# Mixture-of-experts stage of a two-model forward pass: both unit sizes in one block, unrolled groups, tokens as partitions in the small units' down product

## The chip, the cores and the metric

One core of one Trainium2 chip runs the whole program in one launch. The metric is the device time of an execution in microseconds (us). Before the change three runs took 4977.19, 4983.99 and 4990.39 us, median 4983.99 us.

## The reference, cut to what matters

The program is a chain of two small models over 512 tokens of width 1024. The change touches one layer of the first: a top-2-of-8 mixture of SwiGLU experts, in float32, each expert 1024 by 3584.

```python
def moe_swiglu(h, w_router, w_gate, w_up, w_down):
    xt = h.reshape(b * t, d)                              # 512 x 1024
    top_logits, top_idx = lax.top_k(xt @ w_router, 2)     # of 8
    gates = jax.nn.softmax(top_logits, axis=-1)
    order = jnp.argsort(top_idx.reshape(-1))
    xs = xt[order // 2]                                   # 1024 rows, by expert
    hid = (jax.nn.silu(lax.ragged_dot(xs, w_gate, sizes))
           * lax.ragged_dot(xs, w_up, sizes))             # 3584 wide
    ys = lax.ragged_dot(hid, w_down, sizes)               # back to 1024
    ...                                                   # weighted sum of each token's two rows
```

## The kernel before, in words

`moe1` (L1701) runs a norm, `route_stage`, then `swiglu_stage` (L1016) twice, each a block of its own with a barrier and its own buffers, then `combine_stage`. The router counts the tokens of each expert and cuts them into **units**. An expert with at most 128 tokens is one unit of size 0 (128 rows, called A here). A larger one becomes units of size 1 (152 rows, B). How many there are is known only on the chip, so every engine reads the count (`units`, L1725) and loops over the units with `Fori`. With these inputs there are 5 units of A and 3 of B: the trace has 70 groups of one form and 42 of the other.

A unit reads all of its expert's weights, 3 x 3584 x 1024 floats, in 14 **groups** of 256 hidden columns. A group has 1 MB of gate weights, 1 MB of up weights and 1 MB of down weights, in one of two buffers `b`. `groups` (L1041) is an inner `Fori` of seven turns of two groups. For one group:

- SP waits until the buffer is free (`freed[b]`, given by TensorE after the group's last matmul) and issues three DMAs (L1062 to L1064). They add 48 to `loaded[b]`.
- TensorE waits for `loaded[b]`, then for each half j of 128 hidden columns runs the gate and up products over 8 slices of width (L1093) into banks 4 to 7. Here the weights are the stationary operand and `xu`, the unit's rows turned so that width lies in partitions, moves with 128 or 152 columns. Each float32 `matmul` of the program is two TensorE records and two weight-load records in the trace.
- ScalarE applies silu (L1125), VectorE multiplies by the up product (L1141) and so makes `hid[j]`.
- TensorE multiplies down (L1100): for each j eight matmuls with a 128 x 128 piece of `wd` stationary and `hid` moving, into banks 0 to 3, two of them per bank, the output transposed (width in partitions). Zero matmuls (L1076) open these banks at the start of a unit, because they are filled with start=False.

Around the groups stands the **boundary** of a unit. After the last group VectorE copies the four banks to `yT` (L1148), TensorE turns them back to rows (L1112), VectorE copies them to `yrow` (L1684), ScalarE's queue stores them to DRAM (L1689) and waits until they have landed. The next unit begins with `ExpertRows.turn` (L1664, the gathered rows are turned on TensorE) and `place` (L1675, VectorE copies them into `xu` with the norm's gain). POOL's `fetch` (L1647 the index list, L1651 the gather of rows) runs a unit ahead: it waits only for the turn of the unit before.

The order within a queue is the program's. The lines that the change and the steps of the prediction touch:

```python
with sp.Fori(0, units(sp)) as u: ...                                # L1052
sp.wait_ge(freed[b].sem, freed[b].at(u * per[b] + i))               # L1057
pe.wait_ge(loaded[b].sem, loaded[b].at((u * per[b] + i + 1) * 48))  # L1087
```

The dense feed-forward stage `ffn_stage` is used for comparison. It has the same three loads per group but 256 rows at a time, its groups are written out without a loop, and its down product (L1242) has `hid` stationary and 512 columns of `wd` moving.

Of the kernel before, what the change touches and what calls it, by code (L numbers as in the profile page):

```python
# [22 lines left out]
P = 128  # L23
T = 512
TT = T // P
D = 1024
# [11 lines left out]
ROWS_MAX = (FIRST_ROW[1] + UNITS_MAX[1] * UNIT_ROWS[1] + P - 1) // P * P  # L38
LEVELS = 7
# [145 lines left out]
def settle(eng, passed):  # L185


    eng.sem_inc(passed.sem, 1)
# [822 lines left out]
def row_parts(rows):  # L1011

    return [(r0, min(P, rows - r0)) for r0 in range(0, rows, P)]


def swiglu_stage(S, name, letter, rows, hidden, units, weights, x_of, gather, emit):  # L1016

    nc, ps = S.nc, S.ps  # L1020
    n_groups = hidden // GROUP
    per = ((n_groups + 1) // 2, n_groups // 2)
    subs = row_parts(rows)
    per_unit = 2 * len(subs)
    sig = lambda x: S.sig(letter + x)
    loaded = [sig("loaded0"), sig("loaded1")]
    hidden_ready = [sig("hidden0"), sig("hidden1")]
    gate_up, gated = [sig("gate_up0"), sig("gate_up1")], [sig("gated0"), sig("gated1")]
    freed = [sig("freed0"), sig("freed1")]
    y_ready, y_taken, y_turned, emitted, zeros_ready = (  # L1030
        sig(x) for x in ("y_ready", "y_taken", "y_turned", "emitted", "zeros"))
    with ExitStack() as st:
        wg = S.sb(name + "_wg", [P, 2, KD, GROUP], F32, st)
        wu = S.sb(name + "_wu", [P, 2, KD, GROUP], F32, st)
        wd = S.sb(name + "_wd", [P, 2, 2, D], F32, st)
        gated_sb = S.sb(name + "_gs", [P, 2, rows], F32, st)
        hid = S.sb(name + "_hid", [P, 2, rows], F32, st)
        yT = S.sb(name + "_yt", [P, KD, rows], F32, st)
        zero = S.sb(name + "_zero", [P, BANK], BF16, st)

        def groups(eng, u, body):  # L1041

            with eng.Fori(0, n_groups // 2) as i:
                for b in range(2):
                    body(i, b)
            if n_groups % 2:
                body(n_groups // 2, 0)

        with nc.Block(name) as block:
            @block.sync  # L1050
            def _(sp):
                with sp.Fori(0, units(sp)) as u:  # L1052
                    g, up, dn = weights(sp, u)

                    def body(i, b):

                        sp.wait_ge(freed[b].sem, freed[b].at(u * per[b] + i))  # L1057
                        f = (i * 2 + b) * GROUP
                        gv = g[:, bass.ds(f, GROUP)].rearrange("(k p) f -> p k f", p=P)
                        uv = up[:, bass.ds(f, GROUP)].rearrange("(k p) f -> p k f", p=P)  # L1060
                        dv = dn[bass.ds(f, GROUP), :].rearrange("(j p) d -> p j d", p=P)
                        sp.dma_start(wg[:, b, :, :], gv).then_inc(loaded[b].sem, 16)  # L1062
                        sp.dma_start(wu[:, b, :, :], uv).then_inc(loaded[b].sem, 16)
                        sp.dma_start(wd[:, b, :, :], dv).then_inc(loaded[b].sem, 16)  # L1064
                    groups(sp, u, body)

            @block.tensor
            def _(pe):
                pe.wait_ge(zeros_ready.sem, zeros_ready.at(1))
                with pe.Fori(0, units(pe)) as u:  # L1070
                    if gather is not None:
                        gather.turn(pe, u)

                    pe.wait_ge(y_taken.sem, y_taken.at(u))
                    for b in range(4):
                        nc.tensor.matmul(ps[b][:, :], zero[:, 0:P], zero[:, :], start=True, stop=False,  # L1076
                                         skip_group_check=True)
                    if gather is None:
                        pe.wait_ge(emitted.sem, emitted.at(per_unit * u))
                    else:  # L1080
                        pe.wait_ge(gather.x_ready.sem, gather.x_ready.at(per_unit * (u + 1)))

                    settle(pe, S.sig("passed_pe"))

                    def body(i, b):
                        pe.wait_ge(loaded[b].sem, loaded[b].at((u * per[b] + i + 1) * 48))
                        n = u * n_groups + i * 2 + b  # L1087
                        for j in range(2):

                            pe.wait_ge(hidden_ready[j].sem, hidden_ready[j].at(n))  # L1090
                            for w, bank in ((wg, 4 + j), (wu, 6 + j)):
                                for k in range(KD):
                                    last = nc.tensor.matmul(ps[bank][:, 0:rows], w[:, b, k, j * P:(j + 1) * P], x_of(k, u),  # L1093
                                                            start=(k == 0), stop=(k == KD - 1))
                            last.then_inc(gate_up[j].sem, 1)
                        for j in range(2):
                            pe.wait_ge(hidden_ready[j].sem, hidden_ready[j].at(n + 1))
                            for d in range(KD):
                                at = (d % 2) * rows
                                last = nc.tensor.matmul(ps[d // 2][:, at:at + rows], wd[:, b, j, d * P:(d + 1) * P],  # L1100
                                                        hid[:, j, :], start=False, stop=False, skip_group_check=True)
                        last.then_inc(freed[b].sem, 1)
                    groups(pe, u, body)
                    nc.tensor.matmul(ps[3][0:32, 0:2], zero[:, 0:32], zero[:, 0:2], start=False, stop=True,
                                     skip_group_check=True).then_inc(y_ready.sem, 1)
                    pe.wait_ge(y_taken.sem, y_taken.at(u + 1))
                    pe.wait_ge(hidden_ready[0].sem, hidden_ready[0].at((u + 1) * n_groups))
                    pe.wait_ge(hidden_ready[1].sem, hidden_ready[1].at((u + 1) * n_groups))
                    for s, (r0, n) in enumerate(subs):
                        for half in range(2):  # L1110
                            for kk in range(4):
                                last = nc.tensor.transpose(ps[4 + 2 * s + half][0:n, kk * P:(kk + 1) * P],  # L1112
                                                           yT[:, 4 * half + kk, r0:r0 + n], S.const("ident"))
                            last.then_inc(y_turned.sem, 1)

            @block.scalar
            def _(act):
                with act.Fori(0, units(act)) as u:
                    def body(i, b):
                        n = u * n_groups + i * 2 + b  # L1120
                        for j in range(2):
                            act.wait_ge(gate_up[j].sem, gate_up[j].at(n + 1))

                            act.wait_ge(hidden_ready[j].sem, hidden_ready[j].at(n))
                            nc.scalar.activation(gated_sb[:, j, :], ps[4 + j][:, 0:rows], ACT.Silu).then_inc(gated[j].sem, 1)  # L1125
                    groups(act, u, body)
                    if gather is not None:
                        gather.store(act, u)

            @block.vector  # L1130
            def _(dve):
                nc.vector.memset(zero[:, :], 0.0).then_inc(zeros_ready.sem, 1)
                with dve.Fori(0, units(dve)) as u:
                    if gather is not None:
                        gather.place(dve, u)

                    def body(i, b):
                        n = u * n_groups + i * 2 + b
                        for j in range(2):
                            dve.wait_ge(gated[j].sem, gated[j].at(n + 1))  # L1140
                            nc.vector.tensor_tensor(hid[:, j, :], gated_sb[:, j, :], ps[6 + j][:, 0:rows],  # L1141
                                                    ALU.mult).then_inc(hidden_ready[j].sem, 1)
                    groups(dve, u, body)
                    dve.wait_ge(y_ready.sem, y_ready.at(u + 1))

                    dve.wait_ge(y_turned.sem, y_turned.at(per_unit * u))
# [4 lines left out]
                    if gather is not None:  # L1151
                        gather.before_emit(dve, u)
# [1753 lines left out]
```

## Time and profile before

| | us |
|---|---|
| runs | 4977.19, 4983.99, 4990.39 |
| the profiled execution, its own time | 4991.39 |
| its span, first to last instruction | 4989.7 |
| TensorE busy over the span | 3590.2 (72%) |
| VectorE, ScalarE, POOL busy | 1889.2, 579.9, 1363.7 |
| router's blocks end, expert stage begins | about 1484 |
| first and last weight load of the expert stage on TensorE | 1501.3 to 2876.7 |
| combine's first gather | 2885.67 |

The profile cuts the span in 40 slices of 124.7 us. The expert stage fills slices 12 to 22, in which TensorE's digit is 9 but for one. What follows it, slices 23 to 39, is the second model, which the change does not touch.

### The profile page before, as it was taken

The page shows a single profiled execution, that of the slowest core. Times are in us where ns is not written, and L with a number is a line of the kernel's source. Part 1 is how long each engine was busy: PE and PEld are TensorE (multiplying, and loading weights), DVE is VectorE, ACT ScalarE, POOL GpSimd, SP SyncE. Part 2 cuts the span into 40 slices and gives each one's busy share as a digit, 9 for nine tenths or more (in the row PEclk, how much of TensorE's full clock was granted, in tenths as well). Part 3 has the DMA queues.
Part 4 walks back from the last instruction along what each step waited for, and adds up shares of the span by engine and source line. Part 5 has one row for each costly group of instructions (what it writes and reads, how often), then busy time and mean ns, then how long its engine had stood idle before and what let it go on. Part 6 is the DMA issues. An engine that isn't in the chain of part 4 may idle for free. (4 is left out here: it accounts for less than half of the span.)

```text
span 4989.7 us, 48641 instructions
## 1 busy us (share of the span) xinstructions
PE 3590.2 (72%) x18469; PEld 2608.9 (52%) x18469; DVE 1889.2 (38%) x3706; ACT 579.9 (12%) x1313; POOL 1363.7 (27%) x1167
## 2 busy tenths in 40 slices
PE   7969999997569999998999959966065055046036
PEld 3455777645439999998999934643022022012012
DVE  2051230115710000000000031728787777777764
ACT  1121000122301010100000011421011011001001
POOL 0020000002310000000000000004777877877875
PEclk9969999898779999998999979788587578578579
DMA  3112774210138788876776721016899999999998
GB/s 107 51 38 94 247 244 154 88 68 1 39 144 278 271 278 287 274 269 229 253 244 237 247 88 51 1 72 235 291 367 353 327 360 352 322 351 371 327 354 349
DMA packets 533096, 1086.83 MB, mean 218 GB/s; under 512 B 36950, under 2 KB 317808, under 8 KB 532864
## 3 DMA queue, kind: packets, MB, share of 16 engines
q1 hardware_dynamic: 378100, 522.81, 30.7%
q0 software_dynamic: 150544, 545.64, 29.8%
q10 hardware_dynamic: 4348, 17.07, 0.8%
q8 instruction: 56, 0.92, 0.1%
q14 instruction: 48, 0.39, 0.0%
HBM read 1064.14 MB, written 21.28 MB: 218 GB/s over the span
## 5 line engine op out<-in xcount | busy, mean ns | idle before, releaser
L2408 PE MATMUL bank<-peer_ring,peer_diag 128*128 128x512 f32 x1024 | 519.8, 657 | 938.9 <-ACT peer_diag L2505 559.3
L2408 PEld LDWEIGHTS bank<-peer_ring,peer_diag 128*128 128x128 f32 x1024 | 203.1, 208 | 1255.2 <-ACT peer_diag L2505 891.7
L2268 POOL DMA_INDIRECT peer_ring<-in_peer_u_dram,peer_expert x512 | 666.2, 1301 | 686.4 <-DVE peer_expert L2582 486.5
L2647 DVE SCALAR_TENSOR_TENSOR peer_ring<-peer_ring,h_rows 128x1024 f32<-128x1024 f32 x512 | 596.7, 1222 | 177.3 <-DMA peer_ring<-in_peer_u_dram,peer_expert 176.0
L2268 POOL DMA_INDIRECT peer_ring<-in_peer_v_dram,peer_expert x512 | 549.5, 1073 | 160.8 <-issue 154.9
L1141 DVE TENSOR_TENSOR experts_hid<-experts_gs,bank 128x128 f32<-128x128 f32 (+1 forms) x224 | 66.6, 297 | 1216.3 <-ACT experts_gs L1125 1216.3
L1093 PE MATMUL bank<-rows_xt,experts_wg 128*128 128x128 f32 (+1 forms) x3584 | 470.3, 285 | 14.3 <-DMA experts_wd<-in_moe_w_down_dram 13.8
L1093 PE MATMUL bank<-rows_xt,experts_wu 128*128 128x128 f32 (+1 forms) x3584 | 460.3, 282 | 0.0
L1093 PEld LDWEIGHTS bank<-rows_xt,experts_wg 128*128 128x128 f32 x3584 | 446.6, 194 | 24.6 <-issue 24.6
L1100 PE MATMUL bank<-experts_hid,experts_wd 128*128 128x128 f32 (+1 forms) x3584 | 442.0, 282 | 0.0
L1093 PEld LDWEIGHTS bank<-rows_xt,experts_wu 128*128 128x128 f32 x3584 | 440.1, 191 | 0.0
L1100 PEld LDWEIGHTS bank<-experts_hid,experts_wd 128*128 128x128 f32 x3584 | 431.9, 191 | 0.0
L2694 DVE SCALAR_TENSOR_TENSOR peer_acc<-peer_ring,peer_wgt,peer_acc 128x1024 f32<-128x1024 f32 x256 | 328.9, 1285 | 211.5 <-DMA peer_ring<-in_peer_v_dram,peer_expert 203.0
L401 PE MATMUL bank<-xT,proj_w 128*128 128x512 f32 (+2 forms) x736 | 325.0, 600 | 9.0 <-PEq L215 9.0
L1647 POOL DMA_DIRECT2D rows_index<-token_of_row x11 | 6.3, 572 | 991.8 <-PE bank L1664 664.6
L846 POOL TENSOR_TENSOR hgrn_both<-k,hgrn_diff 128x256 f32<-128x256 f32 x56 | 50.5, 908 | 827.2 <-ACT hgrn_diff L791 804.8
L404 PE MATMUL bank<-proj_w,xT 128*128 128x512 f32 (+2 forms) x704 | 265.6, 536 | 0.0
L401 PEld LDWEIGHTS bank<-xT,proj_w 128*128 128x128 f32 (+2 forms) x736 | 136.9, 187 | 190.6 <-issue 189.8
L404 PEld LDWEIGHTS bank<-proj_w,xT 128*128 128x128 f32 x704 | 127.0, 195 | 140.6 <-issue 140.4
L1125 ACT ACTIVATE experts_gs<-bank 128x128 f32<-128x128 f32 (+1 forms) x224 | 63.9, 285 | 966.2 <-PE bank L1093 965.8
L1232 PE MATMUL bank<-xT,ffn_wg 128*128 128x256 f32 x704 | 162.3, 384 | 1.3 <-ACT ada_c L1271 1.3
L1232 PE MATMUL bank<-xT,ffn_wu 128*128 128x256 f32 x704 | 159.1, 379 | 0.0
(421 smaller groups left out, 3446.5 us busy)
## 6 DMA issues: line engine op xcount, KB each, us to landing
experts_wg<-in_moe_w_gate_dram SPq DMA_DIRECT2D x112, 1024.0 KB, 5.2
experts_wu<-in_moe_w_up_dram SPq DMA_DIRECT2D x112, 1024.0 KB, 7.7
experts_wd<-in_moe_w_down_dram SPq DMA_DIRECT2D x112, 1024.0 KB, 9.4
ada_w<-in_w_ada_dram SPq DMA_DIRECT2D x12, 2048.0 KB, 8.0
ffn_wg<-in_ffn_w_gate_dram SPq DMA_DIRECT2D x22, 1024.0 KB, 6.8
ffn_wu<-in_ffn_w_up_dram SPq DMA_DIRECT2D x22, 1024.0 KB, 9.5
ffn_wd<-in_ffn_w_down_dram SPq DMA_DIRECT2D x22, 1024.0 KB, 11.6
proj_w<-in_c_w_in_dram SPq DMA_DIRECT2D x8, 2048.0 KB, 9.2
```

Of the source, the lines that this page charges most:

```text
L401: last = nc.tensor.matmul(out_of(g), wk[:, m * P:m * P + width], xT[:, k, :], start=(k == 0), stop=(k == KD - 1))
L404: last = nc.tensor.matmul(out_of(g), xT[:, k, m * P:(m + 1) * P], wk[:, 0:n], start=(k == 0), stop=(k == KD - 1))
L846: nc.gpsimd.tensor_tensor(halves(both[:, n % 2, :], l)[0], halves(k(p), l)[0], halves(diff[:, p % 2, l, :], l)[0], ALU.mult).then_inc(mixe ...
L1093: last = nc.tensor.matmul(ps[bank][:, 0:rows], w[:, b, k, j * P:(j + 1) * P], x_of(k, u), start=(k == 0), stop=(k == KD - 1))
L1100: last = nc.tensor.matmul(ps[d // 2][:, at:at + rows], wd[:, b, j, d * P:(d + 1) * P], hid[:, j, :], start=False, stop=False, skip_group_c ...
L1125: nc.scalar.activation(gated_sb[:, j, :], ps[4 + j][:, 0:rows], ACT.Silu).then_inc(gated[j].sem, 1)
L1141: nc.vector.tensor_tensor(hid[:, j, :], gated_sb[:, j, :], ps[6 + j][:, 0:rows], ALU.mult).then_inc(hidden_ready[j].sem, 1)
L1232: last = nc.tensor.matmul(ps[bank][:, 0:ROWS], w[:, b, k, j * P:(j + 1) * P], xT[:, k, u * ROWS:(u + 1) * ROWS], start=(k == 0), stop=(k = ...
L2268: pool.indirect_dma_start(out=ring[:, b, :], out_offset=None, in_=tables[phase], in_offset=bass.IndirectOffsetOnAxis(ap=G.expert[:, t, i * ...
L2408: last = nc.tensor.matmul(ps[hf][:, :], diag[:, b // 2, :], ring[:, b, hf * 512:(hf + 1) * 512], start=False, stop=(b == B - 1), skip_grou ...
L2647: nc.vector.scalar_tensor_tensor(ring[:, b, :], ring[:, b, :], 1.0, h2[:, t, :], ALU.mult, ALU.mult, accum_out=dots[:, b:b + 1]).then_inc( ...
L2694: nc.vector.scalar_tensor_tensor(acc[:, :], ring[:, b, :], wgt[:, i * B + b:i * B + b + 1], acc[:, :], ALU.mult, ALU.add).then_inc(weighed ...
```

## The change

One block replaces the two. All buffers of both sizes are allocated together, with one set of weight buffers, and SP goes from the last unit of A to the first of B without a barrier; for B it waits that A's groups have freed the buffer too. The inner loop is gone on all engines but SP: the 14 groups of a unit are written out, inside the loop over units. In A the rows of the next unit are turned inside the last group (into banks 2 and 3), one unit beyond the last as well. A's down product has `hid` stationary and 512 columns of `wd` moving, into banks 0 and 1, so its result has tokens in partitions; `yT`, its turning and the zero matmuls are gone in A. In B the next unit's rows are turned before the results are turned back, and the zero matmuls stand in the first group. Stores are no longer waited for unit by unit.

The old `swiglu_stage` is removed whole. New or changed, cut to its core:

```diff
+LISTED = ROWS_MAX + 2 * P
...
     def turn(self, pe, u):
...
         pe.wait_ge(self.gathered.sem, self.gathered.at(16 * len(self.subs) * (u + 1)))
-        pe.wait_ge(self.emitted.sem, self.emitted.at(2 * len(self.subs) * u))
...
     def store(self, act, u):
         for s, (r0, n) in enumerate(self.subs):
-            act.wait_ge(self.emitted.sem, self.emitted.at(2 * len(self.subs) * u + 2 * s + 2))
             act.dma_start(self.R.y[...], self.yrow[0:n, s, :]).then_inc(self.stored.sem, 16)
-        act.wait_ge(self.stored.sem, self.stored.at(16 * len(self.subs) * (u + 1)))
+def experts_stage(S, R):
+    n_groups = E_FF // GROUP
+    per = n_groups // 2
+    last = n_groups - 1
...
+            @block.sync
+            def _(sp):
+                def unit(E, size, u, others=None, n_others=0):
+                    e = expert_values(sp, R.expert[0:1, size, bass.ds(u, 1)], 0, N_EXP - 1)
...
+                    with sp.Fori(0, per) as i:
+                        for b in range(2):
+                            if others is not None:
+                                sp.wait_ge(others.freed[b].sem, others.freed[b].at(n_others * per))
+                                settle(sp, S.sig("passed_sp"))
+                            sp.wait_ge(E.freed[b].sem, E.freed[b].at(u * per + i))
...
+                            sp.dma_start(wg[:, b, :, :], gv).then_inc(E.loaded[b].sem, 16)
+                            sp.dma_start(wu[:, b, :, :], uv).then_inc(E.loaded[b].sem, 16)
+                            sp.dma_start(wd[:, b, :, :], dv).then_inc(E.loaded[b].sem, 16)
+                n_a, n_b = A.units(sp), B.units(sp)
+                with sp.Fori(0, n_a) as u:
+                    unit(A, 0, u)
+                with sp.Fori(0, n_b) as u:
+                    unit(B, 1, u, A, n_a)
...
+            @block.tensor
+            def _(pe):
+                n_a, n_b = A.units(pe), B.units(pe)
+                A.turn(pe, 0)
+                with pe.Fori(0, n_a) as u:
+                    pe.wait_ge(A.x_ready.sem, A.x_ready.at(2 * u + 2))
+                    for g in range(n_groups):
+                        b = g % 2
+                        pe.wait_ge(A.loaded[b].sem, A.loaded[b].at((u * per + g // 2 + 1) * 48))
+                        gate_up(A, u, g, 0)
+                        gate_up(A, u, g, 1)
+                        if g == last:
+                            A.turn(pe, u + 1)
+                        for j in range(2):
+                            pe.wait_ge(A.hidden[j].sem, A.hidden[j].at(u * n_groups + g + 1))
+                            if g == 0 and j == 0:
+                                pe.wait_ge(A.y_taken.sem, A.y_taken.at(u))
+                            for hf in range(2):
+                                ins = nc.tensor.matmul(ps[hf][:, :], hid[:, j, 0:P], wd[:, b, j, hf * 512:(hf + 1) * 512],
+                                                       start=(g == 0 and j == 0), stop=(g == last and j == 1))
+                        ins.then_inc(A.freed[b].sem, 1)
+                B.turn(pe, 0)
+                pe.wait_ge(A.y_taken.sem, A.y_taken.at(n_a))
+                pe.wait_ge(A.x_ready.sem, A.x_ready.at(2 * n_a + 2))
+                pe.wait_ge(zeros.sem, zeros.at(1))
+                with pe.Fori(0, n_b) as u:
+                    pe.wait_ge(B.x_ready.sem, B.x_ready.at(4 * u + 4))
+                    for g in range(n_groups):
...
+                        if g == 0:
+                            pe.wait_ge(B.emitted.sem, B.emitted.at(4 * u))
+                            for bank in range(4):
+                                nc.tensor.matmul(ps[bank][:, :], zero[:, 0:P], zero[:, :], start=True, stop=False,
+                                                 skip_group_check=True)
...
+                    B.turn(pe, u + 1)
+                    pe.wait_ge(B.y_taken.sem, B.y_taken.at(u + 1))
+                    for s, (r0, n) in enumerate(B.subs):
+                        for half in range(2):
+                            for kk in range(4):
+                                ins = nc.tensor.transpose(ps[2 * s + half][0:n, kk * P:(kk + 1) * P],
+                                                          yT[:, 4 * half + kk, r0:r0 + n], S.const("ident"))
+                            ins.then_inc(B.y_turned.sem, 1)
...
+            @block.scalar
+            def _(act):
+                with act.Fori(0, n_a) as u:
+                    for g in range(n_groups):
+                        silu(A, u, g, 0)
+                        silu(A, u, g, 1)
+                    act.wait_ge(A.y_taken.sem, A.y_taken.at(u + 1))
+                    A.store(act, u)
...
+                with act.Fori(0, n_b) as u:
...
+                    act.wait_ge(B.emitted.sem, B.emitted.at(4 * u + 4))
+                    B.store(act, u)
...
+            @block.vector
+            def _(dve):
+                A.place(dve, 0)
+                with dve.Fori(0, n_a) as u:
+                    for g in range(n_groups):
+                        hidden(A, u, g, 0)
+                        hidden(A, u, g, 1)
+                    A.place(dve, u + 1)
+                    dve.wait_ge(A.freed[1].sem, A.freed[1].at(u * per + per))
+                    dve.wait_ge(A.stored.sem, A.stored.at(16 * u))
+                    for hf in range(2):
+                        ins = nc.vector.tensor_copy(A.yrow[:, 0, hf * 512:(hf + 1) * 512], ps[hf][:, :])
+                    ins.then_inc(A.y_taken.sem, 1)
+                B.place(dve, 0)
+                with dve.Fori(0, n_b) as u:
...
+                    for bank in range(4):
+                        ins = nc.vector.tensor_copy(yT[:, 2 * bank:2 * bank + 2, :], ...)
+                    ins.then_inc(B.y_taken.sem, 1)
+                    B.place(dve, u + 1)
+                    dve.wait_ge(B.stored.sem, B.stored.at(32 * u))
+                    ...                                   # B.yrow copies, each after its y_turned
+            @block.gpsimd
+            def _(pool):
+                n_a, n_b = A.units(pool), B.units(pool)
+                A.fetch(pool, 0)
+                with pool.Fori(0, n_a) as u:
+                    A.fetch(pool, u + 1)
+                B.fetch(pool, 0)
+                with pool.Fori(0, n_b) as u:
+                    B.fetch(pool, u + 1)
```

## Rows read from the trace of the kernel before

**Rows 1.** The page's 40 slices, TensorE's busy tenths.

```profile
PE   7969999997569999998999959966065055046036
```

**Rows 2.** Timeline, a turn of A's inner loop: start, us, engine, line, operation [idle before].

```profile
1543.43 3.65 PEld L1100 LDWEIGHTS bank<-experts_hid,experts_wd 128*128 128x128 f32 x32
...
1547.73 2.05 PE L1093 MATMUL bank<-rows_xt,experts_wg 128*128 128x128 f32 x16 [0.45 <-DMA experts_wd<-in_moe_w_down_dram]
```

**Rows 3.** Timeline, SP's queue, A: the first load of a group.

```profile
1677.59 0.38 SPq L1062 DMA_DIRECT2D experts_wg<-in_moe_w_gate_dram  x1
1688.37 0.37 SPq L1062 DMA_DIRECT2D experts_wg<-in_moe_w_gate_dram  x1
1699.67 0.38 SPq L1062 DMA_DIRECT2D experts_wg<-in_moe_w_gate_dram  x1
...
1840.61 0.38 SPq L1062 DMA_DIRECT2D experts_wg<-in_moe_w_gate_dram  x1
```

**Rows 4.** Timeline, SP's queue, B: the first load of a group.

```profile
2387.81 0.37 SPq L1062 DMA_DIRECT2D experts_wg<-in_moe_w_gate_dram  x1
2400.23 0.38 SPq L1062 DMA_DIRECT2D experts_wg<-in_moe_w_gate_dram  x1
2412.61 0.37 SPq L1062 DMA_DIRECT2D experts_wg<-in_moe_w_gate_dram  x1
```

**Rows 5.** Timeline, the feed-forward stage: two weight loads that follow each other.

```profile
719.15 0.19 PEld L1242 LDWEIGHTS bank<-ffn_wd,ffn_hid 128*128 128x128 f32 x1 [0.24 <-issue]
719.58 0.19 PEld L1242 LDWEIGHTS bank<-ffn_wd,ffn_hid 128*128 128x128 f32 x1 [0.24 <-issue]
```

**Rows 6.** DMA view of 12 us each: 1513:1525, then 1558:1570 (us to landing stands last).

```profile
q8 instruction: 1, 0.02, 0.6%
...
experts_wd<-in_moe_w_down_dram SPq DMA_DIRECT2D x1, 1024.0 KB, 10.7
...
experts_wd<-in_moe_w_down_dram SPq DMA_DIRECT2D x1, 1024.0 KB, 9.4
```

**Rows 7.** The feed-forward stage, 600 to 900: busy time by engine, then the instruction queue.

```profile
600.00:900.00 300.00, 300.00 (x1170) 221.56 (x1169) 59.53 (x97) 11.14 (x29) 0.00 (x0) 1.00 0.57 195
...
q8 instruction: 9, 0.15, 0.2%
```

**Rows 8.** Timeline, a boundary of A, TensorE: its first and its last row.

```profile
1657.90 0.09 PEld L1104 LDWEIGHTS bank<-experts_zero 128*32 128x32 bf16 x1
...
1665.86 2.35 PEld L1093 LDWEIGHTS bank<-rows_xt,experts_wg 128*128 128x128 f32 x16 [0.63 <-issue]
```

**Rows 9.** DMA view: small transfers, us from issue to landing.

```profile
router_w<-in_moe_router_dram SPq DMA_DIRECT2D x1, 32.0 KB, 2.2
rows_index<-token_of_row POOLq DMA_DIRECT2D x8, 0.5 KB, 4.8
```

**Rows 10.** Timeline, from A's block to B's, TensorE's rows.

```profile
2308.21 0.09 PEld L1104 LDWEIGHTS bank<-experts_zero 128*32 128x32 bf16 x1
...
2335.11 4.30 PEld L1093 LDWEIGHTS bank<-rows_xt,experts_wg 128*128 128x128 f32 x16 [0.28 <-issue]
```

**Rows 11.** Timeline, a boundary of B: TensorE's and VectorE's rows.

```profile
2511.51 0.09 PEld L1104 LDWEIGHTS bank<-experts_zero 128*32 128x32 bf16 x1 [0.16 <-issue]
...
2511.81 1.62 DVE L1148 COPY experts_yt<-bank 128x304 f32<-128x304 f32 x4 [3.69 <-PE bank L1104]
...
2513.66 1.96 PE L1112 MATMUL bank<-consts,experts_yt 128*128 128x128 f32 x16 [1.97 <-DVE experts_yt L1148]
2514.35 2.47 DVE L1684 COPY rows_y<-bank 128x512 f32<-128x512 f32 x4 [0.92 <-PE bank L1112]
...
2516.97 1.67 PE L1664 MATMUL bank<-consts,rows_x 128*128 128x128 f32 x16 [1.35 <-DVE rows_y L1684]
2517.63 1.62 DVE L1675 TENSOR_TENSOR rows_xt<-bank,columns 128x512 f32<-128x512 f32 x4 [0.81 <-PE bank L1664]
...
2519.89 2.11 PEld L1093 LDWEIGHTS bank<-rows_xt,experts_wg 128*128 128x128 f32 x16 [0.78 <-issue]
```

More of the change, by code:

```diff
@@ L1005, in head_norm_stage @@
             s.base += n
[L1011 to L1146, printed above, removed]
-                    for b in range(4):
-                        ins = nc.vector.tensor_copy(yT[:, 2 * b:2 * b + 2, :],
-                                                    ps[b][:, 0:2 * rows].rearrange("p (d r) -> p d r", d=2))
-                    ins.then_inc(y_taken.sem, 1)
-                    if gather is not None:
-                        gather.before_emit(dve, u)
-                    for s, (r0, n) in enumerate(subs):
-                        for half in range(2):
-                            dve.wait_ge(y_turned.sem, y_turned.at(per_unit * u + 2 * s + half + 1))
-                            emit(u, s, half, ps[4 + 2 * s + half][0:n, :]).then_inc(emitted.sem, 1)
-            if gather is not None:
-                @block.gpsimd
-                def _(pool):
-                    with pool.Fori(0, units(pool)) as u:
-                        gather.fetch(pool, u)
@@ L1483, in route_stage @@
         token_i = S.sb("router_token", [P, TT], I32, st)
-        zero_rows = S.sb("router_zero", [1, ROWS_MAX], I32, st)
+        zero_rows = S.sb("router_zero", [1, LISTED], I32, st)
         blank = S.sb("router_blank", [P, D], F32, st)
@@ L1631, in __init__, with units @@
         self.rows, self.row0 = UNIT_ROWS[size], FIRST_ROW[size]
-        self.xg = S.sb(f"rows{size}_x", [P, 2, D], F32, st)
+        self.subs = [(r0, min(P, self.rows - r0)) for r0 in range(0, self.rows, P)]
+        self.bank0 = (2, 4)[size]
+        n = len(self.subs)
+        self.xg = S.sb(f"rows{size}_x", [P, n, D], F32, st)
         self.xu = S.sb(f"rows{size}_xt", [P, KD, self.rows], F32, st)
-        self.yrow = S.sb(f"rows{size}_y", [P, 2, D], F32, st)
-        self.index = S.sb(f"rows{size}_index", [P, 2], I32, st)
-        self.subs = row_parts(self.rows)
+        self.yrow = S.sb(f"rows{size}_y", [P, n, D], F32, st)
+        self.index = S.sb(f"rows{size}_index", [P, n], I32, st)
         self.indexed, self.gathered = (S.sig(f"e{size}_{x}", pool_dma=True) for x in ("indexed", "gathered"))
         self.turned, self.stored, self.x_ready = (S.sig(f"e{size}_{x}") for x in ("turned", "stored", "x_ready"))
-        self.emitted = S.sig(f"s{size}_emitted")
+        sig = lambda x: S.sig(f"s{size}_{x}")
+        self.loaded, self.freed = [sig("loaded0"), sig("loaded1")], [sig("freed0"), sig("freed1")]
+        self.hidden, self.gate_up, self.gated = ([sig(x + "0"), sig(x + "1")] for x in ("hidden", "gate_up", "gated"))
+        self.y_taken = sig("y_taken")
+        if size:
+            self.y_ready, self.y_turned, self.emitted = sig("y_ready"), sig("y_turned"), sig("emitted")
+    def units(self, eng):
+        size = 0 if self.row0 == 0 else 1
+        return expert_values(eng, self.R.units[0:1, size:size + 1], 1, UNITS_MAX[size])
     def fetch(self, pool, u):
-        S, nc, R = self.S, self.S.nc, self.R
-        pool.wait_ge(self.turned.sem, self.turned.at(2 * len(self.subs) * u))
+        S, nc, R, n_subs = self.S, self.S.nc, self.R, len(self.subs)
+        pool.wait_ge(self.turned.sem, self.turned.at(2 * n_subs * u))
         settle(pool, S.sig("passed_pool"))
@@ L1663, in turn @@
                     c = (4 * half + kk) * P
-                    last = nc.tensor.transpose(S.ps[4 + 2 * s + half][:, kk * P:kk * P + n], self.xg[0:n, s, c:c + P],
+                    last = nc.tensor.transpose(S.ps[self.bank0 + 2 * s + half][:, kk * P:kk * P + n], self.xg[0:n, s, c:c + P],
                                                S.const("ident")[0:n, 0:n])
@@ L1711, in moe1 @@
         R.y = nc.dram_tensor("y_rows", (ROWS_MAX, D), F32, kind="Internal").ap()
[L1712 removed]
+        R.token_of_row = nc.dram_tensor("token_of_row", (LISTED, 1), I32, kind="Internal").ap()
         norm_stage(S, "norm3", S.gains[:, 3, :], xn_dram=R.xn)
         route_stage(S, R)
[L1715 to L1726 removed]
+        experts_stage(S, R)
         combine_stage(S, R)
```

105 lines of the change are left out of this document (85 added, 20 removed).

## The prediction, made before the changed kernel was run

> **What bounds the kernel now.** I read the page's slices first, to place the stage: TensorE is at nine tenths through it [rows 1]. The gain has to come from what still lies between its matmuls, so I then read three timelines.
>
> Inside A's inner loop the 32 weight loads of a down product take 3.65 us [rows 2]. Taking off the last one's own 0.19 [rows 5] leaves a step of 0.112, so the 96 records of a group are 10.72 us. In SP's queue the first loads of successive groups stand 10.78 and 11.30 us apart, 22.08 for two groups [rows 3]. Two groups of matmuls are 21.44, so TensorE waits 0.64 per pair. The wait is named as one for the down weights [rows 2]. In B the same two steps are 12.42 and 12.38 [rows 4], which is the bare matmul time of 152 columns, with only 0.04 at the loop's edge. So the edge of the short loop is almost free, and A's 0.64 is the weight load's latency. A buffer is refilled only after its own group has ended, and is needed one group later. From the end of a group to the moment when the next group of that buffer may start passes 10.72 + 0.64 = 11.36 us. A therefore runs at the pace "one group's matmuls plus 11.36" per pair, and what shortens a group by x brings x per pair, not 2x.
>
> The boundaries are the rest: 8.0 us in A [rows 8], 8.4 in B [rows 11], and 26.9 from A's last product to B's first, because the second block loads weights and gathers rows from nothing [rows 10].
>
> **Part by part.**
>
> *A's down product.* Eight records of 512 columns instead of 32 of 128. In the feed-forward stage such records start 0.43 us apart [rows 5], so 3.44 instead of 3.57: a group becomes 10.59, a unit's fourteen 148.3.
>
> *The unrolled body.* The feed-forward stage is written out, and in 300 us it drew nine packets of 16 KB on the instruction queue for 1170 + 1169 TensorE records [rows 7], one per 260 records. A unit of A becomes 14 x 144 + 16 = 2032 records, 8 packets, and with its waits I take 9; a unit of B (2720) takes 11. What a packet does to a load can be read: a load of A during which one instruction packet ran landed its down weights after 10.7 us, one without after 9.4 [rows 6]. That is 1.3 us, on the very latency that sets A's pace. With an ordinary load the wait per pair is 11.36 - 10.59 = 0.77, with one hit by a packet 2.07. Seven pairs all ordinary wait 5.4, all hit 14.5; with nine of fourteen hit, 11.2. About 1.0 of it disappears beside the turn and the edge at the boundary, which leaves 10.2. B has 12.38 per group against 11.36 for a load: an ordinary load costs nothing, a hit one (12.66, and 0.1 for SP's second wait) 0.4 per pair, at most 2.7 a unit. I take 1.8, or 5.4 for three units.
>
> [...]
>
> *The far edge.* At the end of a unit's body TensorE now branches back over some 130 KB. No row shows such a branch. The near one costs 0.04 [rows 4], which is the lower bound; the upper is the landing of a small DMA under load, 4.8 us, while a small one alone lands in 2.2 [rows 9]. The records queued ahead of the branch cover part of it. I take 1.5, and keep 0 and 5. [...]
>
> *A's boundary.* Next rows are turned inside the last group: eight transposes, half of the 16 that take 1.67 [rows 11], 0.9 with their fill. VectorE's `place` and its two copies lie beside the last down product and the next gate products. Queued behind ScalarE's new wait for `y_taken` are the store and the next unit's first silu, wanted 3.6 us into the unit, while the copies end after 1.8; nothing is late. POOL has fetched those rows a unit earlier. A unit's period becomes 148.3 + 0.9 + 10.2 + 1.5 = 160.9, against 1840.61 - 1677.59 = 163.0 [rows 3]. Four boundaries save 8.4. The last unit, to its last product, goes from 163.0 - 8.0 = 155.0 to 159.4, which costs 4.4; the first saves 0.4 of zero matmuls. **A: -4.4.**
>
> *From A to B.* SP loads B's first groups during A's last, and the rows are there, since POOL runs ahead. What is left is B's turn (1.7) beside VectorE's two copies (about 1.4), then `place` (1.62) [rows 11], with semaphores 3.5. **-23.4.**
>
> *B.* After the last product the turn (1.67) runs beside the four copies (1.62), then the result's transposes (1.96): about 4.2 with the steps between, while `place` ends earlier [rows 11]. The zero matmuls move into the first group but stay, 1.0, and the far edge adds 1.5: 6.7 against 8.4, twice: -3.4. In the first unit the zero matmuls were inside the old gap: +1.0. TensorE's clock had dropped over that gap: the first 16 weight loads took 4.30 instead of 2.11 [rows 10, 11]; after a pause of 2 us I let 0.5 of it stay: -1.7. With the 5.4 above, **B: +1.3.**
>
> *Ends.* After the last unit `place` runs once more for nothing ahead of the copies to `yrow`, and the first store now waits for all four copies (2.47) [rows 11]; against the transposes that it overlaps, +2.0. At the start every queue reads one more value; no row shows one alone, I bound it by 0 and the 2.2 of a small transfer and take 0.6. The longer list to clear ends beside other router work: 0. **+2.6.**
>
> Sum: -4.4 - 23.4 + 1.3 + 2.6 = **-23.9**. The profiled execution took 4991.4 and would take 4967.5. It lies 7.4 above the median of the runs, so against 4984.0 the forecast is **4960**.
>
> **The rivals.**
>
> 1. *Instruction packets cost the loads nothing*, because they fall into gaps of the load queue. Then A's units wait 4.4 instead of 10.2 (29.0 for five) and B's 5.4 go: -58, 4926. For it: only the part of a load in which its data move can be hit. Against it: the 1.3 us seen in [rows 6], and nine packets in 160 us can't all fall there.
> 2. *The far edge costs the whole of a loaded small DMA*, 5 us: 3.5 more at six edges is 21, leaving -3: 4981, no change. For it: it comes when SP has just started a load. Against: records queued ahead, and a load that would otherwise be waited for.
> 3. *Slower: the sequencers stall on each block of code.* A unit of A asks for its blocks twice as fast as the feed-forward stage did, and VectorE's and ScalarE's bodies are written out too. Five units of 9 and three of 11 are 78 blocks; at 1.3 us each +101, 5061. It decides from (23.9 + 15) / 78 = 0.5 us a block. Against it: TensorE was busy 300.00 of 300.00 us through nine such blocks [rows 7].
>
> That the change doesn't do what it says would show as B's first group still waiting for rows or weights. POOL's extra fetch for A stands ahead of B's, but it waits only for a turn that is a unit old, so I give this nothing of its own.
>
> **How the numbers follow.** A measurement of this kernel tells 0.3% (15 us) from no change. Forecast 0.6, rival 1 0.2, rival 2 0.12, rival 3 0.08. The forecast's own range comes from the edge (0 to 3: -9 to +9) and from 7 to 12 hits a unit in A (-6 to +8): 4946 to 4975. For 8 in 10 I reach toward rival 1 and to rival 2: 4922 to 4982. Faster by over 0.3% means under 4969: rival 1 and most of the forecast, 0.73; within, the rest and rival 2, 0.19; slower 0.08.
>
> **What would show it.** In the profile of the changed kernel: under 5 us between A's last product and B's first; pairs of A's groups at about 22.6 where packets hit and 21.95 where none does, instead of 22.08; eight or nine instruction packets in a unit of A, with the down weights' landing at 10.7 in those loads; 512-column records 0.43 apart; after each unit of A a pause of 0 to 5 us ahead of its first gate product. I am wrong if A's pairs stand at 21.4 or less (then the load wasn't the bound), if landings stay at 9.4 throughout, or if TensorE waits in the middle of a group.

## The result and the profile after

The changed kernel took 5006.94 us (median of five runs, 4999.11 to 5012.03) against 4984.42 for the kernel before beside it: a ratio of 1.0044, 95% interval 1.0027 to 1.0061. It is slower by 0.4%, where 0.5% faster was forecast. The profiled execution took 5002.58, its span is 5000.8.

The page's slices again first. The dip between the two blocks is gone, the rest of the row looks as in [rows 1]:

```profile
PE   7969999997559999999999959976055045046036
```

The expert stage runs from VectorE's first instruction in it to POOL's first gather of the combine. Timeline of the kernel before, those two rows (start, us, engine, line, operation, idle before):

```profile
1484.36 0.27 DVE L1132 MEMSET experts_zero<- 128x256 uint32 x1 [15.31 <-PEq L1486]
...
2885.67 0.97 POOL L1741 DMA_INDIRECT combine_y<-y_rows,row_of  x1 [358.30 <-PEq L1736]
```

and the same of the changed kernel:

```profile
1480.75 0.27 DVE L1688 MEMSET experts_zero<- 128x256 uint32 x1 [15.02 <-PEq L1333]
...
2897.61 0.96 POOL L1771 DMA_INDIRECT combine_y<-y_rows,row_of  x1 [185.82 <-PEq L1766]
```

The stage grew from 1401.3 to 1416.9 us, by 15.6. The time ahead of it is 3.6 shorter, and the time after it is the same, 2104.0 and 2103.2. This length is the measure used for the experiments below, each from one execution. It stays comparable when a kernel runs on another chip, where the second model takes longer (2166 us after the stage in the first experiment).

**What was won is there.** Timeline of the changed kernel, from A's last down product to B's first gate product:

```profile
2329.15 3.60 PE L1611 MATMUL bank<-experts_wd,experts_hid 128*128 128x512 f32 x8
...
2336.22 2.33 PE L1590 MATMUL bank<-rows_xt,experts_wg 128*128 128x152 f32 x16 [1.99 <-DVE rows_xt L1532]
```

The product ends at 2332.75, B begins 3.5 us later instead of 26.9 [rows 10], at a granted clock of 1.00 (2.33 for 16 records).

**What was lost stands at each unit's start.** Timeline of the changed kernel, TensorE and SP, from one unit of A to the next:

```profile
1655.98 3.60 PE L1611 MATMUL bank<-experts_wd,experts_hid 128*128 128x512 f32 x8
...
1661.88 0.97 PEld L1590 LDWEIGHTS bank<-rows_xt,experts_wg 128*128 128x128 f32 x8 [3.13 <-issue]
...
1667.61 1.78 PEld L1590 LDWEIGHTS bank<-rows_xt,experts_wg 128*128 128x128 f32 x8 [4.76 <-issue]
1669.28 3.53 PEld L1590 LDWEIGHTS bank<-rows_xt,experts_wu 128*128 128x128 f32 x16
```

The last down product ends at 1659.6. After 2.3 us eight records of the next unit run, then TensorE stands for another 4.6 (its weight queue 4.76) in the middle of the product over the slices of width. No instruction of the program waits there; the releaser is "issue", nothing that the profile shows. What follows runs at half speed: 16 weight loads take 3.53 us, not 1.87. The windows view of the same kernel (length, then each engine's busy time, PEclk third from the end) shows a granted clock of 0.95 of full speed over the eight records, and of 0.50 through the second pause and until 1672.6:

```profile
1661.90:1663.00 1.10, 1.10 (x8) 0.95 (x8) 0.00 (x0) 0.00 (x0) 0.88 (x1) 0.95 1.08 384
1663.00:1667.60 4.60, 0.05 (x1) 0.00 (x0) 0.00 (x0) 0.00 (x0) 0.00 (x0) 0.50 0.99 335
1667.60:1672.60 5.00, 4.99 (x23) 4.99 (x24) 0.00 (x0) 0.00 (x0) 0.00 (x0) 0.50 1.03 407
```

The whole first group of the unit therefore stands 20.6 us long in SP's queue (from 1659.82 to 1680.44), against 10.6 for one without a pause: this edge costs 10.0 us, the other three of A 9.8, 11.9 and 9.8. The trace records an instruction packet (one on the DMA queue that the profile names instruction) that runs from 1657.9, beside the last down product, to 1660.0 and one from 1665.2 to 1666.1; TensorE resumes 1.9 and 1.5 us behind them, at 1661.9 and 1667.6.

B's edges differ in form: one pause of 5.3 or 5.5 us behind the result's transposes, then 16 records at half speed (4.42 us, not 2.33; granted clock 0.51 and 0.50). Timeline of the changed kernel, TensorE, then SP's queue, one boundary of B, 25.0 us where the kernel before had 21.0 (the other: 25.5 and 22.2):

```profile
2522.18 4.42 PE L1590 MATMUL bank<-rows_xt,experts_wg 128*128 128x152 f32 x16 [5.32 <-issue]
...
2513.05 0.37 SPq L1573 DMA_DIRECT2D experts_wg<-in_moe_w_gate_dram  x1
...
2538.05 0.38 SPq L1573 DMA_DIRECT2D experts_wg<-in_moe_w_gate_dram  x1
```

The DMA view of the changed kernel over the stage has 90 packets on the instruction queue (the kernel before: 4):

```profile
q8 instruction: 90, 1.47, 0.5%
```

and the effect of some on a load is the one of [rows 6]. Stretch 1556.9 to 1567.3, without a packet; then 1680.3 to 1691.7, with one; then 1567.5 to 1578.5, also with one:

```profile
experts_wd<-in_moe_w_down_dram SPq DMA_DIRECT2D x1, 1024.0 KB, 9.4
...
q8 instruction: 1, 0.02, 0.6%
...
experts_wd<-in_moe_w_down_dram SPq DMA_DIRECT2D x1, 1024.0 KB, 10.7
...
q8 instruction: 1, 0.02, 0.6%
...
experts_wd<-in_moe_w_down_dram SPq DMA_DIRECT2D x1, 1024.0 KB, 9.3
```

What differs is when the packet runs. In the loads between 1680 and 1805 us it started 5.1 to 8.2 us behind the load's first DMA where the down weights landed after 10.7 to 10.9 us, and 10.1 to 12.1 us behind it where they landed after 9.4 to 9.6. So in these loads a packet that came 10 us or more behind the first DMA cost nothing.

### The profile page after: what moved, and what is told of

Same layout as the page of the kernel before. It is cut to its first block and busy times, and to the rows that moved or that the text cites. A ratio compares the mean times of both kernels' runs of the same rounds, so it can differ in the third digit from the quotient of the medians.

```text
span 5000.8 us, 44756 instructions
## 1 busy us (share of the span) xinstructions
PE 3580.1 (72%) x16748; PEld 2466.1 (49%) x16748; DVE 1883.8 (38%) x3691; ACT 541.3 (11%) x1283; POOL 1359.8 (27%) x1173
## 3 DMA queue, kind: packets, MB, share of 16 engines
q8 instruction: 142, 2.33, 0.2%
## 5 line engine op out<-in xcount | busy, mean ns | idle before, releaser
L1611 PE MATMUL bank<-experts_wd,experts_hid 128*128 128x512 f32 x560 | 252.0, 593 | 0.0
L1636 PE MATMUL bank<-experts_hid,experts_wd 128*128 128x152 f32 x1344 | 180.5, 293 | 0.0
L1636 PEld LDWEIGHTS bank<-experts_hid,experts_wd 128*128 128x128 f32 x1344 | 176.3, 190 | 0.4
```

Of the source, the lines that this page charges most:

```text
L1611: ins = nc.tensor.matmul(ps[hf][:, :], hid[:, j, 0:P], wd[:, b, j, hf * 512:(hf + 1) * 512], start=(g == 0 and j == 0), stop=(g == last an ...
L1636: ins = nc.tensor.matmul(ps[d // 2][:, at:at + B.rows], wd[:, b, j, d * P:(d + 1) * P], hid[:, j, :], start=False, stop=False, skip_group_ ...
```

## The experiments

Theory after the result: TensorE's unrolled body is too long for its code to stay from one pass to the next. Behind each branch back to the start of a unit the code is fetched again, packet by packet, and the fetching goes on through the unit and lengthens the weight loads. Rivals: the pause is a wait for rows, values or semaphores at the unit's start; or the load's latency alone is to blame.

The chips differ. Beside the first four runs (6 and 12 groups of code, the down product alone, the early loads) the kernel before took 5046.39, beside the other three 4975.47. So times are compared by the ratio to the kernel before on the same chip, and by the stage's length.

### Code for 6 groups

```diff
+                def pairs(head, tail, body):
+                    for p in range(head):
+                        body(p, p == 0, p == per - 1)
+                    if head + tail < per:
+                        with pe.Fori(head, per - tail) as p:
+                            body(p, False, False)
+                    for p in range(per - tail, per):
+                        body(p, p == 0, p == per - 1)
...
-                    for g in range(n_groups):
-                        b = g % 2
...
+                    def pair(p, opens, closes):
+                        for b in range(2):
...
+                    pairs(1, 1, pair)
```

in A and in B, on TensorE alone: the first pair of groups, a loop over five pairs, the last pair.

> The changed kernel, but TensorE's body of a unit is the first pair of groups, a loop over five pairs, and the last pair: code for 6 groups instead of 14 (about 60 KB). Nothing else differs. Theory (code): the pauses after each unit come from fetching code behind a far branch, and the instruction packets lengthen the loads. Then both go: the first gate product of a unit follows the last down product of the one before by under 1 us (2.3 us and then 4.8 us of pause in the changed kernel), pairs of A's groups stand 21.95 us apart, hardly any instruction packet in the stage (90 in the changed kernel), time about 4925 us. Rival 1 (waits): the pause is a wait for rows or values at the unit's start and stays; only the longer loads go, about 4975. Rival 2: six groups of code don't stay resident either, so each turn of the short loop stalls as well: over 5100.

Measured: ratio to the kernel before 0.9914 (0.9885 to 0.9942), stage 1357.3 us, 9 instruction packets. Timeline, a unit edge of A in the kernel with 6 groups of code:

```profile
1650.37 3.60 PE L1620 MATMUL bank<-experts_wd,experts_hid 128*128 128x512 f32 x8
...
1653.81 2.01 PE L1599 MATMUL bank<-rows_xt,experts_wg 128*128 128x128 f32 x16
...
1668.05 3.46 PEld L1599 LDWEIGHTS bank<-rows_xt,experts_wg 128*128 128x128 f32 x16 [4.27 <-DMA experts_wd<-in_moe_w_down_dram]
```

The pauses before and inside the unit's first group are gone: the gate product begins as the down product drains. Rows, values and semaphores are the same as in the changed kernel, so they were not the cause; the first rival falls, and so does the second. The stage is 59.6 us shorter than the changed kernel's. B's boundaries lost their pause too (17.4 us in SP's queue instead of 25). The absolute time that I had expected, 4925, would be a ratio of 0.988, just below the interval; what the last row shows, a new wait, is of that size. The second group of A's later units waits 3.4 to 3.9 us (here its weight queue 4.3) for its down weights and then starts at the low clock (granted 0.54 from 1668.0 to 1671.7), which adds some 1.7 (3.68 us for 16 records, not 1.95): about 21 us over four units. The far branch had hidden it.

### Code for 12 groups, and for 10 and 8

The same edit with head = 1, tail = 4 (12 groups in both sizes), and with tail = 3 in A and 2 in B.

> As the one with code for 6 groups, but the first pair, a loop over two pairs and the last four pairs are written out: code for 12 groups, about 120 KB in A and 155 KB in B. [...]

Measured: ratio 1.0003 (0.9986 to 1.002), stage 1397.0 us, 75 packets. A's 12 groups do not stay, and both sizes pause where they branch back. Timeline, TensorE, a unit edge of A, then one of B:

```profile
1804.33 3.60 PE L1620 MATMUL bank<-experts_wd,experts_hid 128*128 128x512 f32 x8
1808.76 1.15 PE L1599 MATMUL bank<-rows_xt,experts_wg 128*128 128x128 f32 x8 [0.83 <-issue]
1811.39 1.16 PE L1599 MATMUL bank<-rows_xt,experts_wg 128*128 128x128 f32 x8 [1.48 <-issue]
...
2489.92 4.42 PE L1599 MATMUL bank<-rows_xt,experts_wg 128*128 128x152 f32 x16 [5.58 <-issue]
```

Yet it gained 20 us of stage over the changed kernel; A's two pauses were 0.6 to 0.8 and 1.5 to 1.6 us at three of its edges, instead of 2.3 and 4.6. At the edge shown the clock stayed up (PEclk 1.00 from 1804 to 1814); behind the other two it was at 0.50 for 2 us (1649 to 1651, 1973.6 to 1975.6). Why a body a little shorter pauses so much less was not tried. One difference stands in the traces: the packet that ends the second pause starts 0.7 us behind the first DMA of the next load here (1808.88, 1808.16), and 5.4 us behind it in the changed kernel (1665.20, 1659.82). Whether the load holds the packet up was not tested.

> As with code for 6 groups, but code for 10 groups in A (about 95 KB) and for 8 in B (about 100 KB). 6 groups (60 KB in A, 75 KB in B) stayed resident, 12 (115 KB in A) did not. If the limit lies near 110 KB, both bodies stay: under 15 instruction packets in the stage, no pause at unit edges, stage 1357 us as with 6 groups. If it lies between 75 and 95 KB, packets are about 75 and each unit edge pauses as with 12 groups: stage about 1395.

Measured, in a single execution (4948.01 us): stage 1383.4 us, 31 packets, between the two cases. The two sizes parted. TensorE's rows at an edge of A, then at one of B:

```profile
1795.28 3.60 PE L1620 MATMUL bank<-experts_wd,experts_hid 128*128 128x512 f32 x8
1798.71 1.95 PE L1599 MATMUL bank<-rows_xt,experts_wg 128*128 128x128 f32 x16
...
2464.09 1.88 PE L1599 MATMUL bank<-rows_xt,experts_wg 128*128 128x152 f32 x6 [5.19 <-issue]
2469.46 2.69 PE L1599 MATMUL bank<-rows_xt,experts_wg 128*128 128x152 f32 x10 [3.48 <-issue]
```

A with 10 groups has no pause, and no packet behind its first unit; B with 8 has two pauses, at a granted clock of 0.50 behind each. How large these bodies are can be estimated from the changed kernel: in the middle of its units a packet of 16 KB (90 in the stage, 1.47 MB) came every 1.73 groups of A and every 1.34 of B, so by this estimate a group has about 9.5 and 12.2 KB. Ten groups of A are 95 KB, eight of B with its turns about 100; six of B (73 KB) had stayed. By this estimate the longest body that ran without fetching had 95 KB of TensorE code, and the shortest that fetched had 100. What sets the limit the runs don't show.

### The down product alone, in the kernel before

```diff
-                            for d in range(KD):
+                            for hf in range(2 if by_token else 0):
+                                last = nc.tensor.matmul(ps[hf][:, :], hid[:, j, :], wd[:, b, j, hf * 512:(hf + 1) * 512],
+                                                        start=False, stop=False, skip_group_check=True)
+                            for d in range(0 if by_token else KD):
```

and no `yT`, its copies or transposes for size 0; `by_token` is true for size 0.

> The kernel before, with one part of the change: size 0's down product has the hidden rows stationary and 512 weight columns moving; its result is copied straight to rows, so the copies to the transposed buffer and their transposes go. Loops and two blocks as before. Theory (a pair of A's groups takes its matmuls once plus the load's latency): pairs go from 22.08 to 21.95 us, that is 4.6 us over 35 pairs, and a boundary of A from 8.0 to about 5 us (15 over five): 4965. Rival (matmuls alone set the pace): pairs fall by 0.27 to 21.81. Rival (512 moving columns are no faster here): 22.08 stays.

Measured: ratio 0.9957 (0.9941 to 0.9973), stage 1381.3 us, 20.0 shorter than before. From A's last down product to the next unit's first gate product 4.3 us pass, where the kernel before had 7.4 to 8.0: a little better than the 5 expected. The pairs fell further than expected: in one unit they are 21.84, 22.02, 21.82, 21.89, 21.85 and 21.85, where the kernel before has 22.12 at the same place. That is 0.25, near the rival's 0.27. Yet TensorE still waits for the down weights (its weight queue 24 times between 1660 and 2310 us, 0.5 each), so matmuls alone don't set the pace either. The down weights' median landing is 9.3 us here and 9.4 in the kernel before; why, the runs don't say.

### Gate and up loads sent early

```diff
-                            sp.wait_ge(E.freed[b].sem, E.freed[b].at(u * per + i))
+                            sp.wait_ge(E.gate_up[1].sem, E.gate_up[1].at(u * n_groups + i * 2 + b - 1))
...
                             sp.dma_start(wg[:, b, :, :], gv).then_inc(E.loaded[b].sem, 16)
                             sp.dma_start(wu[:, b, :, :], uv).then_inc(E.loaded[b].sem, 16)
...
+                            sp.wait_ge(E.freed[b].sem, E.freed[b].at(u * per + i))
+                            settle(sp, S.sig("passed_sp"))
                             sp.dma_start(wd[:, b, :, :], dv).then_inc(E.loaded[b].sem, 16)
```

in the changed kernel, with all its code (for B, the same waits on A's last groups).

> The changed kernel with 14 groups of code, but SP sends the gate and up loads of a group when the gate and up products of the group two before it are done, not when its down product is done; only the down weights wait for that. Theory: A's waits in mid unit are the load's latency lengthened by instruction packets (9.7 us a unit), so they vanish: groups of A 10.59 us apart with or without a packet, about 50 us less, while the pauses after each unit stay at some 10 us: about 4955. Rival (the packets stall TensorE itself): groups still show waits of about 1 us where a packet runs, about 4990 or more.

Measured: ratio 0.9966 (0.9939 to 0.9994), stage 1368.8 us, 48.1 shorter than the changed kernel's, with 90 packets as before. (The stage's 32.5 us against the kernel before would make 0.9936, just below the interval.) Inside A's later units every group is 10.6 us. The edges stay, with pauses of 2.8 to 3.0 and 4.3 to 4.9 us. Timeline, TensorE, the edge and the group after it:

```profile
1808.52 3.60 PE L1617 MATMUL bank<-experts_wd,experts_hid 128*128 128x512 f32 x8
1815.05 1.15 PE L1596 MATMUL bank<-rows_xt,experts_wg 128*128 128x128 f32 x8 [2.93 <-issue]
1820.52 2.07 PE L1596 MATMUL bank<-rows_xt,experts_wg 128*128 128x128 f32 x8 [4.31 <-issue]
...
1831.96 1.95 PE L1596 MATMUL bank<-rows_xt,experts_wg 128*128 128x128 f32 x16
```

So in mid unit the packets did not stall TensorE (10.6 us a group with a packet or without); in the changed kernel they cost there only through the loads. The branch at the edge costs with either order of the loads: from here to the run with both cures the stage loses 58.0 us.

### Both cures

> Both cures together: TensorE's body with code for 6 groups, and the gate and up loads sent when the gate and up products are done. If pauses behind far branches and the load's latency are two separate causes, their gains add: groups of A 10.6 us apart everywhere, including the second group of each unit, which with code for 6 groups alone waited 3.4 us for its down weights and started at a low clock. Expert stage about 1312 us (1401 before, 1417 changed, 1357 with 6 groups, 1369 with early loads), so about 90 us or 1.8% faster than the kernel before. Rival: the loads run into the DMA engines' rate once nothing waits (3 MB per 10.6 us is 297 GB/s, plus 1 MB of rows per unit), and groups grow to 11 us in the first half of each unit: stage about 1330.

The two edits above, code for 6 groups and early loads, stand together. Measured: ratio 0.9846 (0.9816 to 0.9876), that is 1.5% faster than the kernel before (the medians alone, 4889.59 and 4975.47, make 1.7%); stage 1310.8 us against the 1312 expected. Timeline, TensorE, a unit edge of A, and the windows view of the stretch that holds another (PEclk 1.00, TensorE busy throughout, 302 GB/s):

```profile
1785.68 3.60 PE L1626 MATMUL bank<-experts_wd,experts_hid 128*128 128x512 f32 x8
1789.11 1.95 PE L1605 MATMUL bank<-rows_xt,experts_wg 128*128 128x128 f32 x16
```

```profile
1500.00:1650.00 150.00, 150.00 (x1020) 122.64 (x1019) 10.54 (x32) 9.06 (x29) 1.53 (x2) 1.00 0.88 302
```

The two causes are separate and add up to within 2 us: the stage goes from 1416.9 by 59.6 (code) to 1357.3 and by 46.5 (loads) to 1310.8; the other way round by 48.1 and 58.0. The rival, the DMA engines' rate, does not show: A's groups stay at 10.6 but for one of 12.3. This version beats both kernels.

### The gather later

```diff
                 with pool.Fori(0, n_a) as u:
+                    pool.wait_ge(A.freed[0].sem, A.freed[0].at(u * per + 3))
+                    settle(pool, S.sig("passed_pool"))
                     A.fetch(pool, u + 1)
```

in the kernel with 6 groups of code.

> As with code for 6 groups, but POOL fetches A's next rows only after the sixth group of the unit, so that their 0.5 MB does not run beside the loads of the unit's first groups. The wait before the second group of a unit there (3.4 us, with the clock low after it) is put down to the down weights landing late, because 0.5 MB of results and 0.5 MB of gathered rows are moved in the same 12 us. Theory: the wait falls by about the time of 0.5 MB, 1.5 us, in each of A's units after the first; stage about 8 us shorter than 1357. Rival (the results' store alone delays it, or the queues' order): the wait stays at 3.4.

Measured, in a single execution (4946.40 us): the first group of A's later units shrank from 14.2 to 14.6 us to 12.4 to 13.0, by about the 1.5 expected, and the wait behind it from 3.4 to 3.9 us to 1.5 to 2.3. But groups 6 and 7 of each unit, beside which the gather now runs, grew from 10.9 to about 12, and the stage is 1361.6 us. The collision had moved, not gone. That the moved rows delay the weights is shown. What is left of the wait may be the results' store; that, and whether the move pays where the loads have slack, was not tried.

## Why the prediction was wrong

**The step that failed is the far edge.** It was priced at 1.5 us with 0 and 5 as bounds, for six edges. It cost 10.0, 9.8, 11.9 and 9.8 us in A, where four edges at 1.5 had been counted: 35.6 more. In B the boundaries came to 25.0 and 25.5 us where the forecast's own terms make 21.0 - 8.4 + 6.7 = 19.3: 11.9 more. No row of the kernel before showed such a branch; the 1.5 was my choice, and the upper bound one small DMA's landing. Two things were left out of it. In A two packets came, with eight records between the pauses behind them, so TensorE stood twice; and in both sizes the granted clock was 0.50 of full speed behind the pause (0.50 from 1667.6 to 1672.6 in A, 0.51 from 2522.2 to 2526.6 in B), so the next 4 to 5 us of matmuls ran at half speed. The second could have been seen in [rows 10], from which I took it for the gap between A and B and not for the edge. I also let queued records cover part of the branch; the packet did start 1.7 us before the last down product's end (1657.9 and 1659.6), and the pause after it shows 2.3 us left uncovered. The prediction had named a wait of TensorE in the middle of a group as a sign of being wrong, and the second pause is one.

**The instruction packets** were the right mechanism. 90 came, 78 were forecast, and one that runs while the load's data move adds 1.3 us as [rows 6] had said. Their weight was a little too large: between its first and last group a unit of A waited 8.8 us (147.35 for thirteen groups of 10.59 and the turn's 0.9), not 10.2. The sum behind it was also built otherwise than the trace: it let nine packets a unit each cost half of 1.3, while in that unit four came early enough in a load, three of which cost the whole 1.3 and one 0.5. Those three pairs took 23.1 to 23.3 us, one without a hit 21.8, where 22.6 and 21.95 had been named. That the total came out near is in part luck. The run with early loads shows that the packets cost A's groups nothing else. (B's 2720 records are miscounted, about 2760; the 11 packets stay.)

**Pace per pair.** "What shortens a group by x brings x per pair" did not hold in size: the down product alone brought 0.25 for an x of 0.13. The latency I had taken as fixed came out 0.1 shorter.

**A to B**: 3.5 us, as forecast, which brought 23.8. **Ends**: from the last product to the combine 10.4 us instead of 8.6, +1.8 against 2.0. **The down product's 512 columns**: 0.43 a record, as in [rows 5]. **The first unit** began at the low clock (granted 0.50 from 1497 to 1502 us) and lost some 1.7 us that I had not foreseen.

Together, by TensorE's rows: A took 28.6 us more than before where -4.4 was forecast, B 9.5 more where +1.3 was, the way from A to B -23.8 against -23.4, the ends +1.2 against +2.6. That makes +15.6 where -23.9 was forecast, 39.5 apart. The far edges alone are 47.5 of it and the first unit 1.7; the rest came back, 7 of it at A's loads (1.4 a unit). Of the rivals, the second had the right mechanism and no bound that reached the price; the third (a stall at each packet of code) did not happen: in the run with early loads A's later groups are 10.6 us long with a packet or without. A time slower by over 0.3% had been given a chance of 0.08.

What the forecast did not look for is a cost that the edge hid. Once the edge is free, the second group of A's later units waits 3.4 us or more. The next rows, which move beside its weights, are shown to be part of the cause; the results' store, the other half MB, is argued.

## What to carry to other kernels

Before a loop on TensorE is unrolled, add up its code: here the 360 float32 matmuls of ten groups of A are 95 KB (estimated above), and a body of 100 KB and more paid at every branch back (8.7 us of pauses at an edge of B with 8 groups, 6.9 at one of A with 14), and, where a load set the pace, 1.3 us for a packet that ran 5 to 8 us behind its first DMA. Price a pause at its length and at what TensorE then loses at the lower clock, here (granted clock 0.50) another 3 us behind 6.9 us of pauses. A weight buffer whose parts are used up at different times should be refilled part by part: that change of one wait on SP was worth 46 to 48 us of the stage, more than the 23.8 of merging the blocks.

## What the runs showed of the hardware that was not expected

- A TensorE loop with about 95 KB of code (10 groups of A, by the estimate above) ran without fetching once its first pass was over; about 100 KB (8 groups of B) fetched in every pass, and paused twice at each branch back, 5.2 and 3.5 us.
- A body of about 114 KB (12 groups of A) paused 0.6 to 0.8 and 1.5 to 1.6 us at three of its edges, one of about 133 KB (14 groups) 2.3 to 2.4 and 4.2 to 6.2. What makes the difference is open.
- In the changed kernel between 1680 and 1805 us one 16 KB instruction packet that started 5 to 8 us behind the first DMA of a 3 MB load lengthened it by 1.3 us (the down weights landed after 10.7 instead of 9.4), though it moves 0.5% of the load's bytes; one that started 10 to 12 us behind it did not (9.4 to 9.6).
- At the unit edges where TensorE paused (the changed kernel, 12 groups, 10 and 8, early loads) it resumed 1.3 to 2.2 us behind the end of an instruction packet.
